# Group-norm variance of a GLA/RWKV-7 layer in quarters of the TensorE array, with the order of work written anew

## What is computed

```python
y, s_rwkv_new = rwkv7_recurrence(r, w, kr, vr, kk, a, s_rwkv.astype(f32))
mu = jnp.mean(y, -1, keepdims=True)                       # over the 64 channels of a head
var = jnp.mean(jnp.square(y - mu), -1, keepdims=True)
y = ((y - mu) * lax.rsqrt(var + RWKV_GN_EPS)).reshape(B, T, RWKV_WIDTH)
y = y * rwkv_ln_w.astype(f32) + rwkv_ln_b.astype(f32)
bonus = jnp.sum(r * kr * rwkv_r_k.astype(f32), -1, keepdims=True) * vr
o_rwkv = (y + bonus.reshape(B, T, RWKV_WIDTH)) * jax.nn.silu(z_r)
```

## Time and profile before

| | |
|---|---|
| median of 3 runs | 2460.07 us (2459.11 to 2461.88) |
| the profiled execution's own time | 2464.55 us |
| its span, first to last instruction | 2462.8 us |
| granted TensorE clock, mean | 0.98 |
| TensorE matmul busy | 2312.1 us, 94% |
| ScalarE busy | 1449.6 us, 59% |
| VectorE busy | 1237.5 us, 50% |
| GpSimd busy | 568.5 us, 23% |

### The profile page before, as it was taken

How to read it: one execution, slowest core, us unless ns; L and a number is a source line. 1 busy time by engine, 2 the same in 40 slices (tenths; PEclk the granted TensorE clock), 3 DMA queues, 4 the chain that set the end, 5 groups by cost and what they waited for, 6 DMA issues and landing times. The chain is left out here.

```text
span 2462.8 us, 71743 instructions
## 1 busy us (share of the span) xinstructions
PE 2312.1 (94%) x31098; PEld 1734.9 (70%) x31098; DVE 1237.5 (50%) x2329; ACT 1449.6 (59%) x2820; POOL 568.5 (23%) x1069
## 2 busy tenths in 40 slices
PE   3899999999999996887999999999999998999998
PEld 3677777777777774765788878888888885544443
DVE  3333333434333333355777767777777777432222
ACT  6455666666556653641777767767777774543333
POOL 0000000000000000253355555555555555000000
PEclk9799999999999998898999999999999999999999
DMA  5111221222221101212222222222222224454444
GB/s 199 58 51 62 91 84 66 75 70 66 70 83 57 52 35 41 67 49 60 65 73 71 58 59 72 72 69 74 73 73 73 72 80 134 125 160 150 153 152 130
DMA packets 196858, 204.73 MB, mean 83 GB/s; under 512 B 108736, under 2 KB 152064, under 8 KB 192192
## 3 DMA queue, kind: packets, MB, share of 16 engines
q1 hardware_dynamic: 192176, 182.83, 24.9%
q10 hardware_dynamic: 4368, 17.30, 1.9%
HBM read 119.81 MB, written 80.28 MB: 81 GB/s over the span
## 5 line engine op out<-in xcount | busy, mean ns | idle before, releaser
L1639 PE MATMUL r_d<-r_hT,w_hi 128*128 128x256 f16 (+1 forms) x3536 | 591.8, 273 | 16.2 <-DMA r_hT<-scratch_hT 15.0
L568 PE MATMUL d<-hT,w_hi 128*128 128x256 f16 (+1 forms) x3264 | 526.6, 270 | 4.1 <-DVE hT L840 4.1
L1639 PE MATMUL r_d<-r_hT,w_lo 128*128 128x256 f16 (+1 forms) x1768 | 477.7, 272 | 0.0
L568 PE MATMUL d<-hT,w_lo 128*128 128x256 f16 (+1 forms) x1632 | 437.3, 270 | 0.0
L1639 PEld LDWEIGHTS r_d<-r_hT,w_hi 128*128 128x128 f16 x3536 | 338.0, 99 | 89.2 <-issue 27.8
L1600 POOL TENSOR_TENSOR r_inv_tmp<-r_inv 64x30 f32<-64x30 f32 (+14 forms) x480 | 256.1, 534 | 473.7 <-DMA r_inv<-scratch_blocks 437.3
L568 PEld LDWEIGHTS d<-hT,w_hi 128*128 128x128 f16 x3264 | 315.8, 98 | 54.3 <-issue 12.5
L1639 PE MATMUL r_d<-w_hi,r_ops 128*128 128x512 f16 x1056 | 315.7, 380 | 2.4 <-DMA r_ops<-scratch_mr 2.4
L1602 POOL TENSOR_TENSOR r_inv<-r_inv,r_inv_tmp 64x30 f32<-64x30 f32 (+14 forms) x480 | 281.0, 585 | 37.6
L1544 POOL MEMSET r_run_s<- 128x128 f16 x1 | 0.2, 204 | 973.3 <-POOLq L270 973.3
L1639 PE MATMUL r_d<-w_lo,r_ops 128*128 128x512 f16 x528 | 201.0, 381 | 0.0
(11 more groups left out here) (260 smaller groups left out, 4163.4 us busy)
## 6 DMA issues: line engine op xcount, KB each, us to landing
x_tok<-in_x SPq DMA_DIRECT2D x33, 512.0 KB, 4.4
r_ops<-in_x SPq DMA_DIRECT2D x33, 512.0 KB, 4.3
out_y<-r_ops SPq DMA_DIRECT2D x33, 512.0 KB, 2.9
scratch_hT<-hT SPq DMA_DIRECT2D x16, 1024.0 KB, 7.0
r_hT<-scratch_hT ACTq DMA_DIRECT2D x16, 1024.0 KB, 6.9
scratch_mg<-m_hl SPq DMA_DIRECT2D x33, 256.0 KB, 2.0
r_zr<-scratch_zr SPq DMA_DIRECT2D x33, 256.0 KB, 3.4
r_bon<-scratch_bonus SPq DMA_DIRECT2D x33, 256.0 KB, 4.9
```

The lines of the kernel that those rows point to most:

```text
L568: mm = pe.matmul(out, lhs(k, a, w), rhs(k, a, w), start=(n == 0), stop=(n == len(terms) - 1))
L1639: mm = pe.matmul(out, lhs(k, a, w), rhs(k, a, w), start=(m == 0), stop=(m == 3 * KT - 1))
```

## The change

`variance` becomes four quarter products (64x64 weights, 256 columns each) instead of one whole one: the even groups of channels go to one bank and the odd ones to another. A quarter product of an odd group reads the other half of the partitions, so `centred` writes the squares of the odd groups with their halves swapped, which takes two half-partition activations in place of one. `deviation` runs its logarithm and its exponential, and `normed` its product, once for each of the two banks. `headmean` shrinks to 64 columns, and two memsets at the start of the phase go. Semaphore counts follow. All four lists are written anew.

```diff
 PE_BODY = """
-    meet:0 scores:1 centre:0 x12*3 inner:1 unknowns:0 turn:1 -bs x4*2 out x4 advance:0 solve:1 join:1 x4*3 lwa0
-    meet:1 scores:2 out lwa2 variance:0 x6*2 inner:2 unknowns:1 turn:2 x6*2 out x6*2 advance:1 solve:2 join:2
-    x0*4 meet:2 out scores:3 x0*2 kn inner:3 unknowns:2 turn:3 x2*4 out x2 advance:2 solve:3 join:3 x2 centre:1
-    x8*2 meet:3 scores:4 out x8*4 inner:4 unknowns:3 turn:4 xs variance:1 out x10*2 advance:3 solve:4 join:4
-    x10*4 out
+    meet:0 scores:1 centre:0 x12*3 inner:1 unknowns:0 turn:1 variance:0 x4*3 out advance:0 solve:1 join:1 x4*3
+    lwa0 meet:1 scores:2 x6 out x6*3 inner:2 unknowns:1 turn:2 x6*2 lwa2 advance:1 out solve:2 join:2 -bs x0*4
+    meet:2 scores:3 out x0*2 kn inner:3 unknowns:2 turn:3 x2*4 out advance:2 solve:3 join:3 x2*2 centre:1 x8*2
+    meet:3 scores:4 x8 out x8*3 inner:4 unknowns:3 turn:4 xs variance:1 out x10 advance:3 solve:4 join:4 x10*5
+    out
 """.split()
 ACT_BODY = """
-    -taken:x10 -load_h centred:0 taken:x12 odd:0 turned:1 tanh_w out z1:1 join_e:1 keep_y:0 taken:x4 tanh:lw0
-    out tanh:la0 squares:0 tanh:lw2 tanh:la2 deviation:0 odd:1 out turned:2 k_factor taken:x6 z1:2 keep_y:1
-    join_e:2 affine:0 squares:2 out gamma taken:x0 odd:2 turned:3 high:0 rnorm:0 out rnorm:1 z1:3 join_e:3
-    keep_y:2 taken:x2 centred:1 out taken:x8 odd:3 turned:4 out deviation:1 affine:1 z1:4 join_e:4 keep_y:3
-    high:1 out
+    -taken:x10 -load_h -high:1 centred:0 taken:x12 odd:0 turned:1 deviation:0 out tanh_w affine:0 z1:1 keep_y:0
+    join_e:1 taken:x4 tanh:lw0 out tanh:la0 squares:0 high:0 odd:1 turned:2 taken:x6 out tanh:lw2 tanh:la2 z1:2
+    join_e:2 keep_y:1 squares:2 gamma out taken:x0 odd:2 turned:3 rnorm:0 rnorm:1 out k_factor z1:3 keep_y:2
+    join_e:3 taken:x2 centred:1 out taken:x8 odd:3 turned:4 deviation:1 out affine:1 z1:4 keep_y:3 join_e:4 out
 """.split()
 DVE_BODY = """
-    zc:0 masked:1 -mixed:x10 -low:1 even:0 keep_w:1 mixed:x12 -bonus:0 out -r -bonus:1 next:0 join_o:1 mixed:x4
-    out masked:2 zc:1 decay out even:1 keep_w:2 normed:0 next:1 mixed:x6 join_o:2 gated:0 out masked:3 zc:2
-    clamp:0 even:2 mixed:x0 keep_w:3 clamp:1 low:0 out unit:0 unit:1 next:2 join_o:3 k_prime mixed:x2 out
-    masked:4 zc:3 beta -td a mixed:x8 strict:0 out strict:1 even:3 keep_w:4 normed:1 rkk next:3 join_o:4 gated:1
-    kappa out
+    -r masked:1 zc:0 -mixed:x10 even:0 mixed:x12 keep_w:1 -low:1 out normed:0 next:0 gated:0 join_o:1 mixed:x4
+    out masked:2 zc:1 low:0 even:1 keep_w:2 out mixed:x6 next:1 decay join_o:2 -bonus:0 out zc:2 masked:3
+    -bonus:1 clamp:0 even:2 clamp:1 keep_w:3 mixed:x0 unit:0 out unit:1 next:2 k_prime join_o:3 mixed:x2 zc:3
+    out masked:4 beta a -td mixed:x8 even:3 keep_w:4 strict:0 out strict:1 rkk normed:1 next:3 kappa join_o:4
+    gated:1 out
 """.split()
 SP_BODY = """
-    -put_m:1 out -bonus_out out out out get_gate:0 out put_m:0 -inverse_back out out blocks_out blocks_in
-    get_gate:1 out
+    -get_gate:1 -put_m:1 out get_gate:0 out put_m:0 out out -bonus_out out -inverse_back out out blocks_out
+    blocks_in out
 """.split()
...
-                out, m = claim(("variance", tile))
-                pe.wait_ge(yc_ok.sem, yc_ok.at(tile, 4))
-                pe.matmul(out[:, :], headmean[:, :], y_sq[:, :], start=True, stop=True).then_inc(*d_full.up(m))
+                parts = claim_pair(("variance", tile))
+                pe.wait_ge(yc_ok.sem, yc_ok.at(tile, 5))
+                for a, (out, m) in enumerate(parts):
+                    for h in range(2):
+                        rows = hrows(swapped(h, a))
+                        mm = pe.matmul(out[hrows(h), 0:2 * P], headmean[rows, :], b4(y_sq)[rows, a::2, :],
+                                       start=True, stop=True)
+                    mm.then_inc(*d_full.up(m))
...
-                    act.activation(b4(y_sq)[:, k::2], out, ACT.Square).then_inc(*yc_ok.up(tile))
+                    for to, rows in (((slice(0, P), slice(0, P)),) if k == 0 else
+                                     ((hrows(1), hrows(0)), (hrows(0), hrows(1)))):
+                        act.activation(b4(y_sq)[to, k::2], out[rows], ACT.Square).then_inc(*yc_ok.up(tile))
...
-                act.activation(out[:, :], out[:, :], ACT.Ln, bias=const(K_GN)).then_inc(*gr_ok.up(tile))
-                act.wait_ge(gr_ok.sem, gr_ok.at(tile, 1))
-                act.activation(out[:, :], out[:, :], ACT.Exp, scale=-0.5).then_inc(*gr_ok.up(tile))
+                for a in range(2):
+                    out = bank_of(("variance", tile, a))[:, 0:2 * P]
+                    act.activation(out, out, ACT.Ln, bias=const(K_GN)).then_inc(*gr_ok.up(tile))
+                for a in range(2):
+                    out = bank_of(("variance", tile, a))[:, 0:2 * P]
+                    act.wait_ge(gr_ok.sem, gr_ok.at(tile, a + 1))
+                    act.activation(out, out, ACT.Exp, scale=-0.5).then_inc(*gr_ok.up(tile))
...
-                dve.tensor_tensor(y, y, b4(bank_of(("variance", tile))), ALU.mult).then_inc(*post_ok.up(tile))
+                for a in range(2):
+                    y = yT[:, tile % 2, a::2]
+                    r = bank_of(("variance", tile, a))[:, 0:2 * P].rearrange("p (g t) -> p g t", g=2)
+                    dve.tensor_tensor(y, y, r, ALU.mult).then_inc(*post_ok.up(tile))
```

More of the change, by code:

```diff
@@ L117 @@
 NBANK = 4
-SET_SUMS, SET_ALL = 15, 36
+SET_SUMS, SET_ALL = 13, 34
 def nchunks(b):
@@ L1158 @@
                 ROUND_NO[_arg[0], _r % _arg[1]] = len(ROUND_NO)
-        elif _job == "centre":
+        elif _job in ("centre", "variance"):
             for _k in range(2):
                 ROUND_NO[_job, _arg, _k] = len(ROUND_NO)
-        elif _job == "variance":
-            ROUND_NO[_job, _arg] = len(ROUND_NO)
 ROUND_KEYS = list(ROUND_NO)
@@ L1388, in rwkv_phase @@
         sj_ok = sig("stream_state", 8, 2)
-        yc_ok = sig("y_centred", 4, NT)
-        gr_ok = sig("y_rstd", 2, NT)
-        post_ok = sig("post", 7, NT)
+        yc_ok = sig("y_centred", 5, NT)
+        gr_ok = sig("y_rstd", 4, NT)
+        post_ok = sig("post", 8, NT)
         mh_ok = sig("m_high", 1, NT)
@@ L1415, in get_gate @@
                 if tile:
-                    sp.wait_ge(post_ok.sem, post_ok.at(tile - 1, 7))
+                    sp.wait_ge(post_ok.sem, post_ok.at(tile - 1, 8))
                 sp.dma_start(zr[:, :, :], t["zr"][b][:, :, i * P:(i + 1) * P]).then_inc(*zr_in.up(tile))
@@ L1626, in claim @@
                     elif old[0] == "centre":
-                        pe.wait_ge(yc_ok.sem, yc_ok.at(old[1], 2 * old[2] + 2))
+                        pe.wait_ge(yc_ok.sem, yc_ok.at(old[1], 3 * old[2] + 2))
                     elif old[0] == "variance":
-                        pe.wait_ge(post_ok.sem, post_ok.at(old[1], 1))
+                        pe.wait_ge(post_ok.sem, post_ok.at(old[1], old[2] + 1))
                     else:
@@ L1671, in claim_pair @@
             def claim_pair(key):
-                return [claim(key + (k,)) if key[0] == "centre" else claim((key[0], key[1] + str(k)))
+                return [claim(key + (k,)) if key[0] in ("centre", "variance") else claim((key[0], key[1] + str(k)))
                         for k in range(2)]
@@ L2065, in centred @@
                     out = bank_of(("centre", tile, k))[:, 0:2 * P].rearrange("p (g t) -> p g t", g=2)
-                    act.activation(b4(y_sq)[:, k::2], out, ACT.Square).then_inc(*yc_ok.up(tile))
+                    for to, rows in (((slice(0, P), slice(0, P)),) if k == 0 else
+                                     ((hrows(1), hrows(0)), (hrows(0), hrows(1)))):
+                        act.activation(b4(y_sq)[to, k::2], out[rows], ACT.Square).then_inc(*yc_ok.up(tile))
                     act.activation(yT[:, tile % 2, k::2], out, ACT.Copy).then_inc(*yc_ok.up(tile))
             def deviation(tile):
-                out = bank_of(("variance", tile))
                 act.preload_act_table_set(LN_SET)
-                act.wait_ge(d_full.sem, d_full.at(ROUND_NO["variance", tile], 1))
-                act.activation(out[:, :], out[:, :], ACT.Ln, bias=const(K_GN)).then_inc(*gr_ok.up(tile))
-                act.wait_ge(gr_ok.sem, gr_ok.at(tile, 1))
-                act.activation(out[:, :], out[:, :], ACT.Exp, scale=-0.5).then_inc(*gr_ok.up(tile))
+                act.wait_ge(d_full.sem, d_full.at(ROUND_NO["variance", tile, 1], 1))
+                for a in range(2):
[5 more added lines that the diff above has]
+                    act.activation(out, out, ACT.Exp, scale=-0.5).then_inc(*gr_ok.up(tile))
             def affine(tile):
                 y = yT[:, tile % 2]
-                act.wait_ge(post_ok.sem, post_ok.at(tile, 1))
+                act.wait_ge(post_ok.sem, post_ok.at(tile, 2))
                 for g in range(4):
@@ L2084, in high_part @@
             def high_part(tile):
-                act.wait_ge(post_ok.sem, post_ok.at(tile, 7))
+                act.wait_ge(post_ok.sem, post_ok.at(tile, 8))
                 if tile:
```

(7 more changed lines are left out.)

8 lines of the change are left out of this document (1 added, 7 removed).

## The result

The changed kernel takes **2490.15 us** (median of 4 runs, 2489.76 to 2492.0) against 2459.59 (2458.59 to 2461.88): ratio 1.0124, 95% interval 1.0107 to 1.0142. It is slower by 30.6 us, where 17.6 had been worked out. The profiled execution lasted 2492.0 us, its span 2490.3, which is 27.5 more than before.

The account below looks back on a forecast made before the run. TensorE's list plus its waits, mainly for VectorE, bounds a pass. 14 full passes at +1.4 us (+19.7) and the other five tiles (-2.1) sum to +17.6: forecast 2478 us, own range 2470 to 2487, whole range 2444 to 2490.

Parts of the forecast that it names:

- first three terms of the sum: Per full pass: variance gain -0.84 us, (A) +0.9, (B) and (C) together +0.9 beyond the old gap.
- R1: Rival: faster, the new order hides the predicted waits; 2446 down to 2433 us; chance 0.24 with its middle cases.
- R2: Rival: no change, 2455 to 2465 us, with half of the waits there; chance 0.12.
- R4: Rival: the variance's quarter products don't overlap, +27 us on top; chance 0.02.
- (A): TensorE's `scores:3` waits for `join_o:2`, placed behind `decay` on VectorE: 0.9 us per full pass.
- (B): TensorE's `scores:4` waits about 1.0 us per full pass for VectorE's `join_o:3`, behind `k_factor` and `k_prime`.
- (C): TensorE's `inner:4` waits 0.85 us, as before, for `td`, now behind `a` on VectorE.
- (D): TensorE's `x10` waits for `strict:0` to free the bank of `xs0`: 0.45 us per full pass.
- (E): TensorE's `scores:2` waits for `join_o:1`, behind `gated:0`; the two within 0.3 us, taken as nothing, 4 us in the range.
- The last passes: Counted only in the variance's gain for the five tiles outside full passes, -2.1 us; no wait in the sum.
- R3: Rival: slower by more, `scores:2` and the last passes also wait, some 9 us on top; 2487 or 2490; chance 0.12.
- The new instructions at nothing: Extra ScalarE and VectorE work for the variance, hidden behind TensorE's `x` pieces: no cost; uncovered, 13 us in all.

Follow-up runs that it names:

- e2_new_lists: The kernel before, with its whole variance, given the four new engine lists of the changed kernel: 2488.99 us, ratio 1.0115.
- e3_join_first: The changed kernel with `join_o:2` put ahead of `decay` on VectorE: 2483.51 us, ratio 1.0095.
- e11_fewer_loads: The changed kernel with ScalarE's logarithm and exponential table loaded only where tanh has replaced it, in the second phase: 2446.75 us, ratio 0.9938.
- e4_join3_first: The changed kernel with `join_o:3` put ahead of `k_prime` on VectorE: 2499.15 us, ratio 1.0150.
- e9_bank_later: The changed kernel with the bank of `xs0` set free only by `strict:1`, one operation later: 2501.38 us, ratio 1.0161.

## Why the prediction was right or wrong

- **Direction and mechanism were right.** The kernel is slower, the variance takes 0.55 us, and the waits stand at the four places named. The first three terms of the sum came within 0.1 us of the typical pass, and of the 30.6 us of loss the quarters themselves make 1.2, not told from nothing, and the new lists the rest (`e2_new_lists`); rivals R1, R2 and R4 fell with the waits and with the 0.55.
- **(A)** was right: 0.95 for 0.9, `join_o` right behind the scans, and `e3_join_first` shows that it stands by itself.
- **(B) and (C)** were right in size (0.97 for 0.9). The sum runs from `join_o:3` through `scores:4` to `td` and does not ask what is left of (C) when (B) is gone, and I later took the two for one chain, which was wrong. `e11_fewer_loads` took (B) away and left (C); `e4_join3_first` took (B) away and doubled (C) and more. Two limits of VectorE lie one behind the other.
- **(D)** had the right bank (`e9_bank_later`) and was too small: 0.61 for 0.45. The step that was off is "`strict:0` starts about 0.25 us after `xs` ends"; it starts 0.43 after the variance has begun, since `mixed:x8`, `even:3` and `keep_w:4` stand ahead of it.
- **(E)**, `scores:2`, was the close place that I took as nothing. My count put the two within 0.3 us of each other; 0.33 came, 4.6 us in all. It goes when ScalarE has fewer loads, and it goes with the whole variance. It is most of what `variance:0` saves just ahead of it, given back: the sum took the gain of 0.42 us in full there, though by its own count `join_o:1` was as late as TensorE.
- **The last passes** were the failed step that counts most: I gave them the share of the variance's gain alone (-2.1, with the opening) and they cost 7.5 us. The term put at nothing was the distance of `variance:0` from `centre:0`, for which "the cover is TensorE's `x` pieces": in the last pass there are no such pieces, TensorE waits 2.9 us for `centred` and then runs at the lower clock, 4.9 us in all, in every version that has `variance:0` early. The other 2.4 us of the 7.5 are open but for their tie to ScalarE. R3 named this place and came to 2487 to 2490, against 2490.15, with a chance of 0.12. Its reason was mostly wrong: it blamed the second bank, but the new lists alone have 5.3 of it (426.7 for 421.4), the second bank in the old lists none (421.1), and both the other 2.2.
- **The new instructions at nothing** held in the full passes: `join_o:1` ends at the same time with them and without (24.95 and 24.91 us after `xs`), and the two logarithms and two exponentials take 1.36 us together for 1.27.
- The range ended at 2490, 0.15 short of the result. It had R3 at its end and no place for R3 and (A) to (D) at their upper ends together.
- The Trainium skill (TensorE: Matmul & The Clock Gate, "Measured speedup vs the span model") has its 3.07 times for four row tiles of K=32 and 512 columns, not for quarters. The 0.7 us that I drew from it is not what the trace shows: four quarters of 256 columns took 0.55 us. No run has one quarter alone, so the factor itself was not measured here.

## What to carry to other kernels

When a product takes one more bank of a rotating set, write down for every claim behind it which reader it now waits for: here a faster product bought such a wait in each order tried. Read every list once more for its last passes, with the items that are missing there struck out: what was covered may stand bare. Cost a hand-made order queue by queue, and after each move ask what the queue does later instead; a wait whose source stands above both places only travels. And look for table loads of a set that is already active: 100 of them cost 26 us in the kernel before and 43 in the changed one, beside the 29 us that the new order costs.

## What was not expected of the hardware

- A table load of the active set costs as much as any: 1.28 us each, 1283 ns in every group. The next activation starts at once (1584.30 + 1.28 = 1585.58, and 1585.59 follows). The Trainium skill (ScalarE: Activation LUTs, "What ACT_TABLE_LOAD costs") has the same 1283 ns and a drain of some 1380 ns for a switch of set. No drain shows between these rows, where the set does not change, nor where it does: before the change the load for the tanh starts at 1548.12, 0.03 us after the activation ahead of it ends (1547.01 + 1.08), and the tanh follows at 1549.41. In all 16 such places of the second phase the two gaps are 0.02 and 0.01 us (medians).
- `xs`, itself in 64x64 tiles, takes 0.93 us to the start of the next product where that is in 64x64 tiles too, and 1.07 where it is 128x128. The Trainium skill (TensorEngine Tiling (Array Packing), "Key Properties") says that a change of tiling mode drains TensorE; it gives no time for it. The difference here is 0.14 us; that it is this drain was not shown.
- TensorE stops for 0.5 to 2.0 us within a group of matmuls, with no releaser in the profile, 1 to 6 times in a run between 1135 and 2050 us, 1.3 to 8.6 us in all (five times before, 7.2 us, and five times after, 6.1). Some stand at the same item in several runs, others do not. That blurs the reading of any one pass, and is why the text uses medians over passes. No run here tells what they are. Three more stops of 1.38 us in the first full pass are waits for VectorE (L2362 before, L2367 after).
